# Four weight pieces of a body move to other slots, and the gather reads a reordered copy of the residual

## The reference, cut to what matters

```
h = rmsnorm(x); q,k,v of two attentions and two gates = h @ W_in
x = x + (sigmoid(g_a) * (A @ W_a) + sigmoid(g_b) * (B @ W_b)) @ W_o
x = x + cross_attention(rmsnorm(x), rmsnorm(mem))
h = rmsnorm(x)
g_prob = softmax(h @ w_grp + b_grp)                 # 4 groups, the best one is kept
e_logits = (h @ w_exp + b_exp) of that group        # 8 experts, the best two are kept
out = sum over the 32 experts of (silu(h @ w_gate) * (h @ w_up) * weight) @ w_down
x = x + out; result = rmsnorm(x, final gain)
```

## Time and profile before

| | |
|---|---|
| median of three runs | 481.56 us |
| the profiled execution's own time | 483.62 us |
| its span, first to last instruction | 481.9 us |
| TensorE busy, weight loads busy | 433.0 us (90%), 333.9 us (69%) |
| VectorE, ScalarE, GpSimd busy | 181.0, 162.1, 39.5 us |
| DMA | 139.53 MB, mean 290 GB/s |
| granted TensorE clock, mean | 0.978 |

### The profile page before, as it was taken

The page is one execution under the profiler, slowest core; times in us unless marked ns, Lnnn a source line. Parts: engine busy times, 40 slices in busy tenths (PEclk is TensorE's granted clock), DMA queues, the critical chain, the costliest instruction groups (busy, mean ns, idle before and its releaser), DMA issues.

```text
span 481.9 us, 7784 instructions
## 1 busy us (share of the span) xinstructions
PE 433.0 (90%) x3097; PEld 333.9 (69%) x3097; DVE 181.0 (38%) x329; ACT 162.1 (34%) x316; POOL 39.5 (8%) x80
## 2 busy tenths in 40 slices
PE   3999999999999999999999898989875877968864
PEld 3999998989999999998967373636451442723621
DVE  3463754756469656455461111111110111101113
ACT  7544657666487444656320101010200100001003
POOL 4010242242000000004020000000000000000000
PEclk9999999999999999999989999999997998989989
DMA  8769874667746855569892999996499999999992
GB/s 301 193 178 266 269 258 139 206 221 220 259 132 199 282 176 175 171 189 360 337 359 113 394 410 408 408 409 240 143 413 410 410 410 409 409 410 409 409 387 90
DMA packets 66228, 139.53 MB, mean 290 GB/s; under 512 B 6646, under 2 KB 40470, under 8 KB 66198
## 3 DMA queue, kind: packets, MB, share of 16 engines
q1 hardware_dynamic: 66192, 139.12, 78.8%
q10 hardware_dynamic: 6, 0.00, 0.0%
HBM read 138.06 MB, written 1.05 MB: 289 GB/s over the span
## 4 chain that ended last, share of the span: by engine, by line
PE 70%; SPq 14%; DMA 10%; issue 2%; ACT 2%; DVE 1%; POOLq 0%; POOL 0%; DVEq 0%; ACTq 0%
PE proj L1166 13%; PE proj L1167 12%; PE proj L1168 12%; PE proj L1401 8%; PE score L1386 6%; SPq L361 6%; DMA moe_slot<-in_expert_w_up_dram 5%; SPq L366 4%; SPq L360 4%; PE score L1425 3%; DMA moe_slot<-in_expert_w_down_dram 3%; PE attno L1433 2%; PE attno L1241 1%; PE probt L1166 1%; PE probt L1168 1%
## 5 line engine op out<-in xcount | busy, mean ns | idle before, releaser
L800 DVE TENSOR_TENSOR w_lo<-w_raw,w_hi 128x1024 fp32r<-128x1024 f32 x66 | 81.2, 1231 | 47.5 <-ACT w_hi L556 47.1
L1401 PE MATMUL proj<-moe_slot,moe_x 128*32 128x512 f32 x512 | 64.8, 657 | 20.4 <-DMA moe_slot<-in_expert_w_up_dram 20.4
L556 ACT ACTIVATE w_hi<-w_raw 128x1024 fp32r<-128x1024 f32 x66 | 69.8, 1059 | 31.5 <-PE proj L1168 25.1
L1166 PE MATMUL proj<-hT_hi,w_hi 128*128 128x256 f32 x232 | 68.2, 294 | 0.0
L1167 PE MATMUL proj<-hT_lo,w_hi 128*128 128x256 f32 x232 | 66.5, 287 | 0.0
L1168 PE MATMUL proj<-hT_hi,w_lo 128*128 128x256 f32 x232 | 66.5, 287 | 0.0
L1386 PEld LDWEIGHTS score<-sel_norm,xres 128*128 128x128 f32 x256 | 60.9, 328 | 3.5 <-issue 1.7
L1386 PE MATMUL score<-sel_norm,xres 128*128 128x128 f32 x256 | 60.2, 394 | 0.2 <-issue 0.2
L1401 PEld LDWEIGHTS proj<-moe_slot,moe_x 128*32 128x32 f32 x512 | 18.0, 119 | 60.7 <-issue 59.8
L754 ACT ACTIVATE silu_g<-proj 128x256 f32<-128x256 f32 x8 | 3.1, 384 | 169.2 <-PE proj L1401 169.2
L1166 PEld LDWEIGHTS proj<-hT_hi,w_hi 128*128 128x128 f32 x232 | 45.5, 196 | 3.2 <-issue 2.0
(11 more groups left out here) (264 smaller groups left out, 744.2 us busy)
## 6 DMA issues: line engine op xcount, KB each, us to landing
moe_slot<-in_expert_w_gate_dram SPq DMA_DIRECT2D x64, 512.0 KB, 14.3
moe_slot<-in_expert_w_up_dram SPq DMA_DIRECT2D x64, 512.0 KB, 15.1
moe_slot<-in_expert_w_down_dram SPq DMA_DIRECT2D x64, 512.0 KB, 14.9
w_raw<-in_w_in_dram SPq DMA_DIRECT2D x34, 512.0 KB, 4.5
w_raw<-in_xattn_wkv_dram SPq DMA_DIRECT2D x8, 512.0 KB, 3.5
w_raw<-in_mix_out_w_dram SPq DMA_DIRECT2D x8, 512.0 KB, 3.4
w_raw<-in_moba_out_w_dram SPq DMA_DIRECT2D x4, 512.0 KB, 4.0
w_raw<-in_swa_out_w_dram SPq DMA_DIRECT2D x4, 512.0 KB, 3.5
```

The source lines that it names most:

```text
L556: act.activation(w_hi[:, g % NS], w_raw[:, g % NW], ACT.Copy).then_inc(hi_done, 1)
L800: dve.tensor_tensor(w_lo[:, g % NS], w_raw[:, g % NW], w_hi[:, g % NS].bitcast(F32), ALU.subtract)\
L1166: pe.matmul(ps, a[0], b[0], start=start, stop=False, skip_group_check=True)
L1401: op = pe.matmul(PJ[0][e * WIN:(e + 1) * WIN, :].rearrange("p (j f) -> p j f", j=2), moe_x[:, k, e * WIN:(e + 1) * WIN], both_w[:, r], sta ...
```

## The change

Four things, in one diff:

1. `slot_of_chunk`: pieces 44 to 47 of a body use slots 9, 10, 11, 12 and no longer 0, 1, 2, 3.
2. A new buffer `xg`, a copy of the residual in the order in which the gather reads it. It lies where `xn` lay. ScalarE writes it with four activations of 128x512 after the squares, reading `xres` with the stride of 16 bytes. The gather and the final part use `xg` where they used `xres`.
3. The place of `xres` becomes slot 21, the place of `h3T` slot 20. Load 20 now waits for `logits_ps`; load 21 for the four copies (`xg_done`) and for both halves of `copy_residual` (`res_copied`). The last squares discard their output into a new place, `junk3`, over dead weights.
4. `copy_residual(1)` moves ahead of the wait for the routing masks. `fin_g` moves from slot 10 to slot 8.

```diff
     def slot_of_chunk(i):
-        return i % SLOTS
+        return i % SLOTS if i < 2 * SLOTS else i - 2 * SLOTS + 9
...
-        xres = sb("xres", [P, TT, D], F32)
+        xres_at = region(8192)
+        xres = sb("xres", [P, TT, D], F32, xres_at)
         xn_at = region(8192)
         xn = sb("xn", [P, TT, D], F32, xn_at)
+        xg = sb("xg", [P, TT, D], F32, xn_at)
...
-        slot_at += [xn_at, sc_at]
+        slot_at += [sc_at, xres_at]
...
-        fin_g = sb("fin_g", [P, D], F32, slot_at[10])
+        fin_g = sb("fin_g", [P, D], F32, slot_at[8])
...
-            sp.wait_ge(sq_done, sq_count(X3_NORM, TT - 1))
+            sp.wait_ge(logits_ps, 1)
             load_experts(20, 0)
-            sp.wait_ge(logits_ps, 1)
+            sp.wait_ge(xg_done, 2 * TT)
+            sp.wait_ge(res_copied, 1)
             load_experts(21, 0)
...
             for t in range(TT):
                 row_squares(X3_NORM, xres, t, 1)
+            act.wait_ge(sq_done, sq_count(X3_NORM, TT - 1))
+            for t in range(TT):
+                for h in range(2):
+                    half = slice(h * (D // 2), (h + 1) * (D // 2))
+                    if KH == 2:
+                        src = xres[:, t, half].rearrange("p (q r) -> p r q", r=RUN)
+                        dst = xg[:, t, half].rearrange("p (r q) -> p r q", r=RUN)
...
+                    act.activation(dst, src, ACT.Copy).then_inc(xg_done, 1)
...
             copy_residual(0)
+            copy_residual(1).then_inc(res_copied, 1)
             pe.wait_ge(c_misc, 17)
             pe.wait_ge(r_mask, 2)
...
-            copy_residual(1)
+            pe.wait_ge(xg_done, 2 * TT)
             pe.wait_ge(trips_set, 1)
...
-                    runs = xres[:].rearrange("p t (h q r) -> p t h r q", h=KH, r=RUN)
                     for k in range(KD):
                         for t in range(TT):
-                            op = pe.matmul(SC[k // 4][:, (k % 4) * P:(k % 4 + 1) * P], runs[:, t, k // RUN, k % RUN],
+                            op = pe.matmul(SC[k // 4][:, (k % 4) * P:(k % 4 + 1) * P], xg[:, t, k * P:(k + 1) * P],
                                            sel_norm[:, t].rearrange("p e s -> p (e s)"), start=t == 0, stop=t == TT - 1)
```

More of the change, by code:

```diff
@@ L200, in hybrid_layer @@
         selw = sb("selw", [P, TT, QE, WIN], F32, r1 + 13312)
+        junk3 = [sb(f"junk3{half}", [P, TT, 512], F32, r1 + (8192, 12288)[1 - half]) for half in range(2)]
         selwT = sb("selwT", [P, T], F32, r1 + 14336)
@@ L313, in hybrid_layer @@
         slots_moved = sem("slots_moved")
+        xg_done, res_copied = sem("xg_done"), sem("res_copied")
         back_ps = [[sem(f"back_ps{t}{half}") for half in range(2)] for t in range(TT)]
@@ L429, in _ @@
                     sp.wait_ge(scaled, t + 1)
-                    sp.dma_start(out[0, t * P:(t + 1) * P, cols], xres[:, t, cols]).then_inc(out_done, 16)
+                    sp.dma_start(out[0, t * P:(t + 1) * P, cols], xg[:, t, cols]).then_inc(out_done, 16)
             sp.wait_ge(out_done, 16 * 2 * TT)
@@ L538, in row_squares @@
             def row_squares(n, rows, t, half):
-                squares(n, rows[:, t, half * 512:(half + 1) * 512], t, half)
+                src = rows[:, t, half * 512:(half + 1) * 512]
+                if n == X3_NORM:
+                    act.activation(junk3[half][:, t], src, ACT.Square, scale=float(D) ** -0.5,
+                                   accum_out=mean_sq[:, n, t, half:half + 1]).then_inc(sq_done, 1)
+                else:
+                    squares(n, src, t, half)
             def unit_hi(n, hi, u):
@@ L738, in _ @@
                 row_squares(X3_NORM, xres, t, 1)
+            act.wait_ge(sq_done, sq_count(X3_NORM, TT - 1))
[5 more added lines that the diff above has]
+                        dst = xg[:, t, half].rearrange("p (r q) -> p r q", r=RUN)
+                    else:
+                        runs = slice(h * (RUN // 2), (h + 1) * (RUN // 2))
+                        src = xres[:, t].rearrange("p (q r) -> p r q", r=RUN)[:, runs]
+                        dst = xg[:, t].rearrange("p (r q) -> p r q", r=RUN)[:, runs]
+                    act.activation(dst, src, ACT.Copy).then_inc(xg_done, 1)
             for t in range(TT):
@@ L763, in _ @@
                     act.wait_ge(back_ps[t][half], total * BODY_QUADS)
-                    squares(4, ACC[t][half][:], t, half, xres)
+                    squares(4, ACC[t][half][:], t, half, xg)
             for t in range(TT):
@@ L767, in _ @@
                 act.wait_ge(rs_done, 2 * 4 + t + 1)
-                act.activation(xres[:, t, 0:512], moe_x[:, 4 * t:4 * t + 4].rearrange("p k s -> p (k s)"), ACT.Copy,
+                act.activation(xg[:, t, 0:512], moe_x[:, 4 * t:4 * t + 4].rearrange("p k s -> p (k s)"), ACT.Copy,
                                scale=rnorm[:, 4, t:t + 1]).then_inc(fin_act, 1)
@@ L1133, in _ @@
                 dve.wait_ge(rs_done, 2 * 4 + t + 1)
-                dve.scalar_tensor_tensor(out=xres[:, t, 512:], in0=ACC[t][1][:], scalar=rnorm[:, 4, t:t + 1],
+                dve.scalar_tensor_tensor(out=xg[:, t, 512:], in0=ACC[t][1][:], scalar=rnorm[:, 4, t:t + 1],
                                          in1=fin_g[:, 512:], op0=ALU.mult, op1=ALU.mult).then_inc(fin_dve, 1)
@@ L1359, in copy_residual @@
                 for t in range(TT):
-                    pe.matmul(ACC[t][half][:], ident[:], xres[:, t, half * 512:(half + 1) * 512], start=True,
-                              stop=True)
+                    op = pe.matmul(ACC[t][half][:], ident[:], xres[:, t, half * 512:(half + 1) * 512], start=True,
+                                   stop=True)
+                return op
             copy_residual(0)
+            copy_residual(1).then_inc(res_copied, 1)
             pe.wait_ge(c_misc, 17)
```

## The result

The changed kernel takes 465.24 us (median of 4 runs, 465.12 to 467.58) beside 482.27 us for the kernel before on the same chip (4 runs): ratio 0.9655, 95% interval 0.9613 to 0.9698. Forecast were 465.8 us and faster.

What follows compares the result with a forecast made beforehand. DMA was taken as the bound from 265 us to the end of the loads; -12.85 (slots) - 3.75 (gather) + 0.85 (copies) = -15.75 us took the median from 481.56 to 465.8 us, range 463.3 to 470.2.

Steps and rivals of the forecast that it cites:

- rival 2: Clock stays half over moved copies, or ScalarE's copies cost as much: first gather 2.7 us late, 467.7 us; chance 0.09.
- The gap at the border: Load stream between bodies 1 and 2, 330 to 350 us: new slots remove the whole stop, -12.85 us.
- The gather: First gather, in quad 1: records every 0.12 us, not 0.229, so 3.8 us and -3.75 us, counted once.
- Rival 1: The gather isn't faster, as load time by columns alone would have it: 469.6 us; chance 0.08.
- The two copies ahead of the count: TensorE's right-half residual copies before the count: count and first gather start 0.85 us later, +0.85 us.
- ScalarE's copies: Four strided copies after the last squares: 0.62 us each, at most 1.06, covered before the exponentials, so 0 us.
- The restart: Stream into used slots after the first gap: data flow from 262.6 us, not 265.5; first load issued near 261.3.
- The tail: From the last piece's landing to the end, 11.9 us: unchanged, at most +0.3 us.
- Rival 3: Ring becomes too short, loads 44 to 47 wait for TensorE in each body: 476.1 or 500 us; chance 0.02.
- Rival 4: The slots do nothing because the gap from 330 to 350 us was something else: 478.7 us; chance 0.03.

Runs made afterwards that it cites:

- the repeat: The changed kernel run again without alteration, in another group of runs, against the kernel before: 467.59 us, ratio 0.9698.
- all five steps: Gather read with steps of 8, 12, 32 bytes in the changed kernel (own step 4; kernel before 16): weight loads 196, 261, 335 ns (192; 328).
- the slots alone: Kernel before with only pieces 44 to 47 in slots 9 to 12 and the final gain in slot 8: 468.89 us, ratio 0.9714.

## Why the prediction was right

The sum was right to 0.1 us (15.75 against 15.85) between the two first profiles. That closeness is luck. The repeat gives 14.29 (226.60 - 212.31), 1.5 us less than forecast, and a median of 467.59, nearer to rival 2's 467.7 than to 465.8, though not by rival 2's way. What the runs bear out is the mechanism and the size to about 1.5 us. Its terms as follows.

- **The gap at the border** (-12.85): seen gone; the stream restarted once and did not stop again. The price of the step in isolation was right too (13.43). What was wrong is silent in the sum: I gave the whole gap to the slots, and either edit closes most of it. The prediction had the numbers for this. It put the end of body 1 at 334.9 instead of 348, but it never asked what the old rule would do with that.
- **The gather** (-3.75): 7.73 us became 3.83 and 7.34 became 3.57, so 3.9 and a pace of 0.112 us where the clock was full; in the repeat, at half clock, 7.73 became 6.66 and only 1.07 was won. Weight loads take 192 ns. Rival 1 is out, and with it the rule by the columns alone from the Trainium skill, "TensorE: Matmul & The Clock Gate", section "LDWEIGHTS (loading the stationary operand)": at equal columns the load took 192 to 335 ns with the step. The cacheline paragraph of the Trainium skill's "SBUF — State Buffer" holds for weight loads at all five steps.
- **The two copies ahead of the count** (+0.85): positions start 7.96 us behind the logits (248.76 - 240.80) and not 7.23 (250.66 in the earlier trace rows), so 0.73; the gather starts 0.94 later (251.15 - 240.80 against 252.84 - 243.43). In the repeat the copies cost nothing (the gather starts 9.23 us behind the logits, 9.41 before), and the gather pays 2.8 us instead. Rival 2 priced a clock that stays low over the copies; what happens there is a clock that falls later, over the gather. That was the one thing missing from the range's reasoning, and the range was wide enough for it.
- **ScalarE's copies** (0): four in 4.13 us, 1.03 each against 0.62 for the squares of the same size with unit steps. The bound of 1.06, by the ratio of the weight loads, was right, and so was the cover, nearly to its edge: the first exponentials start as the copies end, and the second pair still waits 0.52 us for VectorE.

```profile
241.40 4.13 ACT L760 ACTIVATE xg<-xres 128x512 f32<-128x512 f32 x4
...
245.43 0.28 ACT L765 ACTIVATE g_exp<-g_log,g_neg 128x4 f32<-128x4 f32 x1
...
246.61 0.48 ACT L769 ACTIVATE e<-e_top,e_neg 128x1 f32<-128x1 f32 x2 [0.52 <-DVE e_neg L1063]
```

- **The restart** was forecast 2.9 us earlier: the first load into a used slot is issued 17.77 us behind the logits (258.57 - 240.80), before 20.72 (264.15 - 243.43), so 2.95.
- **The tail** (0 to 0.3): 11.85 against 11.87 us. The last gate/up half waited 6.60 us for its data and took 5.05 us.
- **Rival 3**, the shorter ring, is refuted at a distance of 13 and shown at 5. Distances between were not run. Rival 4 is refuted by the slots alone.

## What to carry to other kernels

A gap in a stream of loads has two owners, the distance at which a buffer is used again and the time at which its user is done; mending either can close it, so their gains don't add. Work out each edit's gain with the other one in place and without it. And in a ring whose length does not divide the work, look at the seam: its shortest distance, not its usual one, decides whether the stream can stop. Here a distance of 4 cost 12.85 us with the slow gather and 2.05 with the quick one.

## What the runs showed of the hardware that was not expected

**The dense part has two lengths.** The first profile of the kernel before had 0.21 us per record of the first projections where the changed kernel had 0.12 (chain, first the kernel before, then the changed one):

```profile
13.00 0.21 PE proj L1168
...
16.84 0.21 PE proj L1168
17.05 0.12 PE proj L1166
```

```profile
13.09 0.12 PE proj L1189
13.21 0.12 PE proj L1190
```

In the same instructions TensorE reached its full pace at 17.05 us in the kernel before and by 12.03 in the changed one. The same point of the work (a split of weights on ScalarE) then comes at 32.33 and at 29.70 us, 2.63 apart, and the distance is the same at the logits. It is not the change: the logits began at 240.65 to 241.34 us in seven of the fourteen profiles and at 242.9 to 243.43 in the other seven, and the changed kernel is in both (240.80, and 243.05 in the repeat). What holds the pace down is open, since the granted clock reads 1.00 from 9 to 19 us in both profiles. Medians of few runs can differ by as much as the mix of the two, which is why single terms below 1 us were read from the profiles.

**At half clock a strided gather costs nothing more, a dense one does.** In the profile with the slots alone the granted clock was 0.50 at 252 to 254 us and its gather, with steps of 16 bytes, took 7.36 us, no longer than at full clock (7.34 to 7.73), though the half clock lay over some 2.2 us of it. Its weight loads in that stretch took 329 ns, as at full clock. The dense gather took 6.66 at half clock and 3.83 at full, and its loads 333 ns for 192. First the slots alone, then the repeat:

```profile
L1386 PEld LDWEIGHTS score<-sel_norm,xres x11: 309/329/329, 252.1 to 254.4; 128*128 128x128 f32 x11
```

```profile
L1409 PEld LDWEIGHTS score<-sel_norm,xg x28: 288/333/338, 252.3 to 258.0; 128*128 128x128 f32 x28
```

So part of what the new layout wins is handed back whenever the clock lies low over it.
